# Latent attention: row maxima of the next head begin one step sooner, and stand behind the value products on TensorE

## What is computed

```python
q = (rms_norm_2(c_q, q_norm) @ w_q_up).reshape(B, S, MLA_HEADS, MLA_QK)
kv = (rms_norm_2(c_kv, kv_norm) @ w_kv_up).reshape(B, S, MLA_HEADS, MLA_NOPE + MLA_V)
...
    s = jnp.where(mask, s, -jnp.inf)
    p = jax.nn.softmax(s, axis=-1)
    return jnp.einsum('bhqk,bkhd->bqhd', p.astype(v.dtype), v)
```

## Time and profile before

| | before |
|---|---|
| median of 3 runs | 3157.55 us (3150.29 to 3157.79) |
| the profiled execution's own time | 3158.88 us |
| its span | 3157.1 us |
| mean granted TensorE clock | 0.978 |
| PE busy over the span | 2952.4 us (94%) |
| DVE busy | 1680.0 us (53%) |
| ACT busy | 1213.1 us (38%) |
| POOL busy | 1046.7 us (33%) |

### The profile page before, as it was taken

The page is one execution under the profiler, slowest core; times in us unless marked ns, Lnnn a source line. Parts: engine busy times, 40 slices in busy tenths (PEclk is TensorE's granted clock), DMA queues, the critical chain, the costliest instruction groups (busy, mean ns, idle before and its releaser), DMA issues.

```text
span 3157.1 us, 36649 instructions
## 1 busy us (share of the span) xinstructions
PE 2952.4 (94%) x14426; PEld 2427.1 (77%) x14426; DVE 1680.0 (53%) x1721; ACT 1213.1 (38%) x2001; POOL 1046.7 (33%) x418
## 2 busy tenths in 40 slices
PE   5899999999899999999989999999988889999996
PEld 4788888888678888888767887777766677777785
DVE  4788742113424333434588546677844676566433
ACT  3777700002330111001143333677743456666411
POOL 3222144444344444444433233211213212121352
PEclk9999999999999999999999998999999999999998
DMA  2011131112111111111112211200121211000231
GB/s 104 21 34 36 39 114 47 47 53 101 34 40 49 51 47 47 54 47 47 55 52 87 80 61 64 81 21 21 35 75 38 80 34 34 27 29 26 87 107 67
DMA packets 42571, 171.66 MB, mean 54 GB/s; under 512 B 4464, under 2 KB 5488, under 8 KB 41392
## 3 DMA queue, kind: packets, MB, share of 16 engines
q1 hardware_dynamic: 32976, 119.90, 12.0%
q10 hardware_dynamic: 9440, 49.55, 4.0%
HBM read 143.74 MB, written 25.69 MB: 54 GB/s over the span
## 4 chain that ended last, share of the span: by engine, by line
PE 75%; issue 9%; DVE 9%; ACT 5%; POOL 1%; DMA 0%; ACTq 0%; SPq 0%; POOLq 0%; DVEq 0%
PE ps L562 45%; PE ps L1198 5%; PE ps L960 3%; PE ps L1023 3%; PE aux L1088 3%; PE ps L738 3%; PE ps L1072 2%; PE ob L794 1%; PE ob L1114 1%; PE ob L1117 1%; PE ob L1115 1%; POOL wh L505 1%; PE aux L758 1%; DVE small L2468 1%; PE ob L948 1%
## 5 line engine op out<-in xcount | busy, mean ns | idle before, releaser
L505 POOL TENSOR_TENSOR wh<-raw,con 128x1024 fp32r<-128x1024 f32 x203 | 493.0, 2429 | 2040.2 <-PE ps L562 907.3
L507 POOL TENSOR_TENSOR wl<-raw,wh 128x1024 fp32r<-128x1024 f32 x203 | 546.0, 2690 | 15.9
L562 PE MATMUL ps<-hh,wh 128*128 128x512 f32 x1328 | 415.7, 394 | 19.9 <-POOL wl L507 15.2
L562 PE MATMUL ps<-hl,wh 128*128 128x512 f32 x1328 | 413.1, 392 | 0.0
L562 PE MATMUL ps<-hh,wl 128*128 128x512 f32 x1328 | 413.1, 393 | 0.0
L562 PEld LDWEIGHTS ps<-hh,wh 128*128 128x128 f32 x1328 | 251.4, 190 | 75.6 <-POOL wl L507 16.9
L562 PEld LDWEIGHTS ps<-hh,wl 128*128 128x128 f32 x1328 | 252.0, 190 | 53.0
L562 PEld LDWEIGHTS ps<-hl,wh 128*128 128x128 f32 x1328 | 251.7, 190 | 53.1
L1937 DVE TENSOR_TENSOR px_l<-px,px_h 128x512 fp32r<-128x512 f32 (+3 forms) x288 | 198.6, 692 | 127.8 <-ACT px_h L1751 126.1
L1454 ACT ACTIVATE ff<-fr 128x1024 f32<-128x1024 f32 x32 | 33.9, 1061 | 553.5 <-DVE fr L2191 553.5
L2202 DVE TENSOR_TENSOR y_t<-y_t,ps 128x1024 f32<-128x1024 f32 x120 | 146.4, 1220 | 175.8 <-PE ps L562 175.8
(11 more groups left out here) (452 smaller groups left out, 6367.5 us busy)
## 6 DMA issues: line engine op xcount, KB each, us to landing
raw<-wall SPq DMA_DIRECT2D x211, 512.0 KB, 3.5
spill_x<-x_t ACTq DMA_DIRECT2D x2, 4096.0 KB, 12.4
xold_t<-spill_x ACTq DMA_DIRECT2D x2, 4096.0 KB, 13.3
x_t<-xt SPq DMA_DIRECT2D x8, 512.0 KB, 9.3
spill_o<-op ACTq DMA_DIRECT2D x4, 1024.0 KB, 4.4
o_all<-spill_o ACTq DMA_DIRECT2D x2, 2048.0 KB, 11.3
x_t<-xt ACTq DMA_DIRECT2D x1, 4096.0 KB, 14.5
spill_out<-ot ACTq DMA_DIRECT2D x8, 512.0 KB, 3.0
```

Of the source, the lines that this page charges most:

```text
L505: pool.tensor_tensor(wh[:, s, :, :], raw[:, s, :, :], ones.unsqueeze(1).broadcast_to([P, KT, P]), ALU.mult).then_inc(w_high, 1)
L507: pool.tensor_tensor(wl[:, s, :, :], raw[:, s, :, :], wh[:, s, :, :].bitcast(F32), ALU.subtract).then_inc(w_split, 1)
L562: m = pe.matmul(ps[:, w, a:b], lw[:, sl, k, :], r[:, i, a:b], start=(i == 0 and j == 0), stop=(i == len(ks) - 1 and j == 2))
```

## The change

`LEAD` becomes 6 and a new table, `MLA_AHEAD`, is used by the latent attention on TensorE, ScalarE and VectorE; the other layer's attention keeps `MAX_AHEAD`. With the new table, blocks 0 and 1 are done in step -6 and every later block one step sooner as well. On TensorE the maxima of a step are moved behind the projection pieces and the value products of that step. On VectorE the reductions still stand ahead of the step's low part, and on ScalarE the diagonals still stand behind the step's two exponentials. `ROW_AHEAD` stays. No instruction of the three engines is added or removed.

```diff
-    AV_LAG, LEAD = 2, 5
+    AV_LAG, LEAD = 2, 6
...
     MAX_AHEAD = {-5: (0, 1), -4: (2,), -3: (3,), -2: (4,), -1: (5,), 0: (6,), 1: (7,)}
     ROW_AHEAD = {-2: 0, 2: 1}
+    MLA_AHEAD = {-6: (0, 1), -5: (2,), -4: (3,), -3: (4,), -2: (5,), -1: (6,), 0: (7,)}
...
-    def maxima_of(step, heads):
-
-        h, blocks = of_head(step, MAX_AHEAD, heads, ())
+    def maxima_of(step, heads, ahead=MAX_AHEAD):
+
+        h, blocks = of_head(step, ahead, heads, ())
...
             if 0 <= h < MLA_HEADS:
                 scores(step)
-            for block_of in maxima_of(step, MLA_HEADS):
-                maximum(*block_of)
             hq, k = divmod(step + 1, N_HT)
...
             if step >= AV_LAG:
                 values(step - AV_LAG)
+            for block_of in maxima_of(step, MLA_HEADS, MLA_AHEAD):
+                maximum(*block_of)
             rh, rc = row_of(step, MLA_HEADS)
...
-        def softmax(heads, mx, dgs, sums, row_dst):
+        def softmax(heads, mx, dgs, sums, row_dst, ahead):
...
-                for block_of in maxima_of(step, heads):
+                for block_of in maxima_of(step, heads, ahead):
                     diagonal(*block_of)
...
-        def softmax(heads, mx, sums, ot_free):
+        def softmax(heads, mx, sums, ot_free, ahead):
...
-                for block_of in maxima_of(step, heads):
+                for block_of in maxima_of(step, heads, ahead):
                     maximum(*block_of)
```

More of the change, by code:

```diff
@@ L1806, in _ @@
         act.preload_act_table_set("natural_log_exp_and_others")
-        tile, sums_of, _ = softmax(MLA_HEADS, MLA_MAX, dg, inv, lambda h: qa[h % 2][0][96:P, :])
+        tile, sums_of, _ = softmax(MLA_HEADS, MLA_MAX, dg, inv, lambda h: qa[h % 2][0][96:P, :], MLA_AHEAD)
         def y_high(m):
@@ L1851, in fox_row @@
             return fqb[h % 2][a:a + 32, :]
-        fox_tile, fox_sums, fox_send = softmax(2 * FOX_PAIRS, FOX_MAX, fdg, finv, fox_row)
+        fox_tile, fox_sums, fox_send = softmax(2 * FOX_PAIRS, FOX_MAX, fdg, finv, fox_row, MAX_AHEAD)
         fox_base = t.now("tiles") - 2 * FOX_PAIRS * N_HT
@@ L2523, in ot_read @@
                 dve.wait_ge(g_made, pair)
-        tile, weighted = softmax(MLA_HEADS, MLA_MAX, inv, ot_read)
+        tile, weighted = softmax(MLA_HEADS, MLA_MAX, inv, ot_read, MLA_AHEAD)
         for step in range(-LEAD, MLA_HEADS * N_HT + AV_LAG + 2):
@@ L2591, in forget @@
                     fox_low(piece, 0)
-        fox_tile, fox_weighted = softmax(2 * FOX_PAIRS, FOX_MAX, finv, lambda pair: dve.wait_ge(ot_out, 64 + 16 * pair))
+        fox_tile, fox_weighted = softmax(2 * FOX_PAIRS, FOX_MAX, finv, lambda pair: dve.wait_ge(ot_out, 64 + 16 * pair), MAX_AHEAD)
         fox_base = t.now("tiles") - 2 * FOX_PAIRS * N_HT
```

## The result

The changed kernel is slower: median 3194.5 us (3191.2 to 3196.8), against 3157.7 us for the kernel before. The ratio is 1.0122, with a 95% interval of 1.0110 to 1.0134. The profiled execution has a span of 3194.9 us, 37.8 us more than before, and a mean granted clock of 0.973 against 0.978. The forecast was 3179 us: the sign was right, the size too small by 15.5 us. The result lies above the forecast's own range (3168 to 3192) and inside the one stated for eight times in ten (3158 to 3200).

A forecast was written before the change was run, and what follows sets the result against it. TensorE bounds the kernel but for a stall before maximum(4), within a loop over ACT and DVE. 7 x 2.1 + 3 x 0.4 + 5 = 21 us more gave 3179 us; own range 3168 to 3192, eight in ten 3158 to 3200.

The forecast's parts named there:

- the rival in which POOL also gets in before low(10): On DVE low(10) waits for POOL's wh: stall 4.1 in place of 1.7 us, 17 us more, 3196 us; chance 0.10.
- Item 5, the low keys: VectorE's low keys ka_l come behind POOL's split: new 1.7 us stall before step 0's scores, bounds 0 and 4.1 us.
- In the three heads with a dip they pay 0.4 only: Three heads with a clock dip behind maximum(4): POOL comes late, ka_l gets through, each pays 0.4 us only.
- Items 1 to 4, the loop: Loop of reduction 7, ACT's diagonals, low(7), reduction 3, maximum(4) and PE up to maximum(7): +0.4 us a head.
- item 3: Steps 0 to 4, from reduction 7 through the rotary operations: +0.9 us, some 0.3 of it a new PE wait at latent_kv.
- Item 6, the dips: PE's clock behind the new stalls: three new dips at 1.7 us, 5 us; bounds none and ten (17 us).
- Item 7, the ends: Loop starting one step sooner and head 11 getting its maxima sooner: 0 +- 2 us for both.
- ka_l was not in before POOL: Rival: ka_l gets in before POOL's split, no new stall, only 10 x 0.4 = 4 us remain, 3162 us; chance 0.18.
- The stall at maximum(4) was not removed: Rival: PE's stall at maximum(4) goes, nothing replaces it: 14 us and 5 us of dips saved, 3139 us; chance 0.12.

The follow-up runs named there:

- the half-change with the old table: Half of the change alone: TensorE's maxima stand behind the value products, but the old table MAX_AHEAD is kept; median 3185.6 us, ratio 1.0092.
- the first experiment: The changed kernel with one edit: VectorE makes the next head's low keys ka_l in step 9, not step 10; median 3163.0 us, ratio 1.0021.
- the fastest kernel: The kernel before with VectorE's low values and scaled output put ahead of low(7) in step 7, nothing else changed; 3144.5 us, ratio 0.9961.

## Why the prediction was right on the sign and short on the size

The sum was 21 us over the kernel before, and the span grew by 38. The mechanism that decides, the low keys behind POOL's split, was right; four sizes were too small, all on the same side. That the result is inside the stated range is in part luck: the range reached up to 3200 to take in the rival in which POOL also gets in before low(10), priced at 3196. The measured 3194.5 is close to that price, but low(10) took 0.41 to 0.42 us in all ten heads, so that case did not happen.

- **Item 5, the low keys: right.** The order low(10), POOL, ka_l came as worked out: POOL 0.07 us behind low(10) (0.10 worked out) and 0.26 ahead of ka_l (0.23). The stall was 1.85 us (1.7), the row of ka_l 3.40 us. Ka_l one step sooner, ka_l one step later in the kernel before, and the split released later all confirm the cause. With the rule of the Trainium skill (SBUF — State Buffer, "Who interferes with whom"), that issue order decides who blocks, these traces agree down to 0.03 us (POOL first) and 0.01 us (ka_l first, over wl). The runs also answer what I had left open, who is next when two wait: in the ten meetings of the changed kernel, the ten of the half-change with the old table and the ten of the kernel before with ka_l in step 11, it was the one issued first, although it had not yet been able to start.
- **"In the three heads with a dip they pay 0.4 only": wrong.** All ten heads paid: ten ka_l rows between 3397 and 3411 ns. The step took the dips to stay behind maximum(4) and to delay latent_q alone. Most did not stay there, and the two that did, at 2112 and 2296 us, kept POOL from going first in neither head: they delay both sides, since reduction 5 ahead of ka_l waits for PE as the split does. In the head at 2112 us the split came 4.86 us after maximum(4) and ka_l 5.11, in the head at 2173 us, without a dip, 3.28 and 3.54. That is 3 x (2.1 - 0.4) = 5 us too little.
- **Items 1 to 4, the loop: +0.65 us a head in place of +0.4.** It is seen with ka_l out of the way. Its signs came: maximum(4) waited 0.91 to 1.16 us (I wrote 1.2 to 1.4), scores(9) 0.28 us for px_h (0.4). Of the 0.3 us at latent_kv (item 3) 0.09 to 0.14 came. The waits at maximum(4) and scores(9) together (2.6 us in two heads) are no longer than before (2.8), so most of the 0.65 lies in PE's rows between them. Part of that can be read there, since a matmul ahead of a pause costs its whole time. In the first experiment the mask matmul ahead of scores(9) costs 0.22 us (at 2091.27 us, with 0.27 us of idle time behind it), where such a matmul in a full row of the kernel before costs 0.06 (2177.28 to 2177.34 us). The matmul ahead of latent_kv costs 0.40 us (at 2080.42 us), before it was 0.22 (2166.52 to 2166.74 us). The first matmul behind each of these two new pauses costs some 0.07 us more as well. My estimate from these rows is 0.5 us a head for the two pauses; the rest is not settled. With the stall's 1.85 the 0.65 makes 2.5 of the 2.7 us that a head became longer, where the sum had 2.1: over ten heads 6 us too little, the 0.2 without a name included.
- **Item 6, the dips: three more expected, five more came.** From the first maximum(4) on there were nine in place of four. Seven of ten stalls for ka_l had one, where I had counted three, and two lay at maximum(4), where I had left three. Five at 1.6 us each are 8 us in place of 5, 3 too little.
- **Item 7, the ends: 0 +- 2, and 3.6 came.** 3.1 us are lost ahead of the first maximum(4), with waits of head 0 and a sixth new dip. Of the 4.8 us behind the nine heads 1.3 are neither stall nor dip, and 0.8 of these are the longer loop of the tenth head, counted above. The bound of one stall of 1.6 us for each end left out that such a wait can bring a dip, too. The prediction also passed over the last heads when it said that every wait for a reduction is one before maximum(4): of the 13 waits in the earlier trace rows three, 3.1 us, lie behind the ten, at 2288, 2298 and 2300 us.

These four (the dip heads, the loop, the dips and the ends) make 5 + 6 + 3 + 3.6 = 18 us, about the 17 that the sum was short of the span's 38.

The rivals: ka_l was not in before POOL, except where it was moved there (3163.0 us; the rival's price was 3162). The stall at maximum(4) was not removed. The mechanism I gave for its removal, that ScalarE's exponentials in step 7 must come no later, was only half of it: with DVE's two operations out of the way, a low(7) as late as ever is enough. It starts 23.2 us after the maximum(4) ahead of it in the kernel before (2149.42 - 2126.19) and in the fastest kernel (2114.58 - 2091.36). Low(10) was not blocked.

## What to carry to other kernels

When a matmul moves in PE's list, it moves the releases of all other engines with it; write down which VectorE instruction is queued when GpSimd is released, for here one operation that changed sides of it by 0.3 us cost 31 of 37 us. Work that is ready belongs into an engine's idle time ahead of a wait, not behind it: in the changed kernel with ka_l in step 9 a head took 27.67 us with the two operations behind low(7) and the same with them behind low(8), and 26.4 us with them ahead of low(7). And a reordering meant to remove a stall should be set against the cheapest thing that stands in the loop, which was two operations in another list.

## What was not expected of the hardware

A dip of the clock follows some stalls and not others of the same length: 7 of 10 at about 1.85 us, in the half-change all five of 1.76 us and none of 1.74, and of the waits at maximum(4) two of the five of 1.16 us and none of the five of 0.90. In the kernel before with ka_l in step 11 it was again 7 of the ten stalls, of 2.0 to 2.4 us, and three of these dips were twice as long; that profiled execution took 3203.4 us, the longest of its kernel. Where the stalls were 0.64 us or shorter there was none in ten heads. So my estimate for a new stall of 1.7 to 1.9 us is its length and about 0.7 times 1.6 us more, with a wide bound. And the split on POOL is slowed as well: wl took 3.23 to 3.45 us where ka_l was ahead of it, 2.39 where nothing was. These 0.8 to 1.1 us are less than the 2.2 that ka_l lost behind wh (3.40 against 1.21), and TensorE waited for wl in none of the three kernels.
